# Replacing three-part low-precision products by plain float products in the first stage and in the dense expert stage

## What is computed

```python
proj = jnp.einsum('bld,dc->blc', x, w_in)
z_s, xbc, dt_pre, u_m, v_m, o_m, i_pre, f_pre = jnp.split(proj, offs, axis=-1)
xbc, new_ssd_conv = _causal_conv(xbc, st_ssd_conv, conv_ssd_w, conv_ssd_b)
xbc = jax.nn.silu(xbc)
...
u_c, new_mconv = _causal_conv(u_m, st_mconv, conv_m_w, conv_m_b)
...
def block(xb):                      # experts
    ...
    hid = jax.nn.gelu(jnp.einsum('td,thkd->thk', xb, jnp.take(u, eidx, axis=0)), approximate=False)
    return jnp.einsum('thk,thkd->td', gate * hid, jnp.take(v, eidx, axis=0))
```

## Time and profile before

| what | us |
|---|---|
| median of 3 runs | 3532.05 |
| lowest and highest | 3519.77 and 3536.51 |
| the profiled execution, time on the device | 3519.66 |
| its span from the first to the last instruction | 3517.9 |
| mean granted TensorE clock in it | 0.957 of full |

### The profile page before, as it was taken

The page is one execution under the profiler, slowest core; times in us unless marked ns, Lnnn a source line. Parts: engine busy times, 40 slices in busy tenths (PEclk is TensorE's granted clock), DMA queues, the critical chain, the costliest instruction groups (busy, mean ns, idle before and its releaser), DMA issues.

```text
span 3517.9 us, 45887 instructions
## 1 busy us (share of the span) xinstructions
PE 3159.4 (90%) x15111; PEld 2142.2 (61%) x15111; DVE 2543.4 (72%) x5323; ACT 966.6 (27%) x2280; POOL 1738.2 (49%) x1432
## 2 busy tenths in 40 slices
PE   8998998999788888888878666999999999999998
PEld 8998997878433332223234444777677767777764
DVE  6662001699586888888888995777777777777777
ACT  3112222566201111211148873111111111111111
POOL 2322221344125667766664455555555555565553
PEclk9999999899899999999989887999999999999999
DMA  3324432687857999999998999999999999999996
GB/s 110 92 82 160 161 140 93 225 295 272 313 163 253 361 345 356 362 332 341 360 332 325 338 349 364 381 394 392 392 391 398 395 376 382 397 394 389 391 378 242
DMA packets 393200, 1074.39 MB, mean 305 GB/s; under 512 B 56040, under 2 KB 158440, under 8 KB 385952
## 3 DMA queue, kind: packets, MB, share of 16 engines
q0 software_dynamic: 186624, 679.56, 51.5%
q1 hardware_dynamic: 144728, 308.27, 24.1%
q10 hardware_dynamic: 61640, 84.02, 6.6%
HBM read 978.52 MB, written 93.05 MB: 305 GB/s over the span
## 4 chain that ended last, share of the span: by engine, by line
PE 41%; DMA 11%; DVE 9%; issue 6%; POOL 4%; ACT 1%; POOLq 0%; ACTq 0%; DVEq 0%; another core or an unknown queue 0%; SPq 0%
PE PB L2138 17%; PE PB L2125 14%; DMA vbf<-in_peer_v,gixv 7%; PE PB L2165 3%; PE PB L2114 3%; DVE ub L1794 3%; PE PB L2101 2%; POOL ub L1524 2%; DMA x1d<-in_peer_u 2%; POOL vbf L1524 2%; DMA ub<-in_peer_u,gix 2%; PE PB L2209 1%; PE PB L2083 1%; DVE ohb L1741 1%; DVE oha L1739 0%
## 5 line engine op out<-in xcount | busy, mean ns | idle before, releaser
L1524 POOL DMA_INDIRECT ub<-in_peer_u,gix x640 | 692.0, 1081 | 639.8 <-DVE hid L1794 432.4
L2138 PE MATMUL PB<-vbd,wd 128*128 128x512 f32 x1536 | 685.3, 596 | 0.0
L2125 PE MATMUL PB<-xds,uts 128*128 128x384 f32 x3072 | 569.0, 340 | 0.0
L2125 PEld LDWEIGHTS PB<-xds,uts 128*128 128x128 f32 x3072 | 531.3, 189 | 0.5 <-issue 0.5
L1524 POOL DMA_INDIRECT vbf<-in_peer_v,gixv x300 | 339.7, 1132 | 279.6 <-PE PB L2165 133.1
L1524 POOL DMA_INDIRECT vbf<-in_peer_v,gix x340 | 396.9, 1167 | 163.1 <-issue 100.8
L2138 PEld LDWEIGHTS PB<-vbd,wd 128*128 128x128 f32 x1536 | 283.8, 191 | 309.9 <-issue 309.9
L2165 PE MATMUL PB<-vbf,dg 128*64 128x512 f32 x1200 | 327.1, 669 | 137.5 <-DMA vbf<-in_peer_v,gixv 130.3
L1755 DVE TENSOR_TENSOR uts<-PB,uts 128x512 fp32r<-128x512 f32 x256 | 176.0, 687 | 299.1 <-ACT uts L1971 291.5
L1794 DVE CUSTOM_DVE_ANT_0 ub<-ub,x1g 128x1024 f32<-128x1024 f32 x257 | 313.9, 1223 | 73.0 <-DMA ub<-in_peer_u,gix 60.8
L1971 ACT CAST uts<-PB 128x512 fp32r<-128x512 f32 x256 | 150.0, 586 | 641.2 <-PE PB L2114 619.3
(11 more groups left out here) (398 smaller groups left out, 5304.9 us busy)
## 6 DMA issues: line engine op xcount, KB each, us to landing
vbd<-in_peer_v SPq DMA_DIRECT2D x128, 512.0 KB
x1d<-in_peer_u SPq DMA_DIRECT2D x96, 512.0 KB
gd_d<-stag ACTq DMA_DIRECT2D x12, 2048.0 KB
gbd<-gd_d SPq DMA_DIRECT2D x16, 1536.0 KB
ubd<-in_peer_u SPq DMA_DIRECT2D x32, 512.0 KB
wtr<-in_w_tok SPq DMA_DIRECT2D x12, 1024.0 KB, 6.7
tok_d<-stg ACTq DMA_DIRECT2D x96, 128.0 KB, 1.7
rb<-rows_d SPq DMA_DIRECT2D x8, 1536.0 KB, 9.3
```

Source lines behind the costliest of these rows:

```text
L1524: pool.indirect_dma_start(out=buf, out_offset=None, in_=a[table], in_offset=bass.IndirectOffsetOnAxis(ap=index, axis=0)).then_inc(done, 16)
L2125: last = T.matmul(PB[:, 6, 0:TD], uts[:, b % 2, ul, k, :], xds[:, xl, k, :], start=(k, n) == (0, 0), stop=(k, n) == (KD - 1, 2))
L2138: last = T.matmul(PB[:, 2 * d + n, :], wd[:, b % 2, d * CH:(d + 1) * CH], vbd[b % 8][:, n * 512:(n + 1) * 512], start=b == 0, stop=b == NB ...
```

## The change

In the first stage x is loaded once into `xt` and used as it is, and the weights are used where they were loaded (`wrow`, `wcr`, `wtr`). Each product is one plain float matmul where there were three. The casts on ScalarE, the subtractions on VectorE and the splits on GpSimd are gone. Before a tile TensorE waits for the load, and SP waits for TensorE's last use of a buffer before it loads it again. SP issues the loads of x ahead of the first two channel tiles. ScalarE takes tile j out of the accumulator before it finishes tile j - 1 (`chan_in`, `chan_out`, unrolled), and the sum of the four sample parts is stored two tiles later. In the dense part `uts` holds the transposed u once, as float; `u_low` is gone from VectorE, the copy of x into a high part from ScalarE, and its low part from GpSimd; `block_u` has 8 matmuls instead of 24. The loads of the `v` blocks 4 to 7 wait for `gmm` and no longer for the split of x.

```diff
@@ first stage, SyncE
                     sp.dma_start(wrow, a["w_row"]).then_inc(s_wr, 16)
+                    for k in range(KD):
+                        sp.dma_start(xt[:, k, :], a["x_t"][:, k, :]).then_inc(s_x[k], 16)
                     for q in range(2):
                         sp.dma_start(wcr[q][:, :, :], a["w_ch"][q, :, :, :]).then_inc(s_w[q], 16)
-                    for k in range(KD):
-                        free(sp, s_xl, k - NX + 1)
-                        sp.dma_start(xst[k % NX], a["x_t"][:, k, :]).then_inc(s_x[k % NX], 16)
...
-                                sp.wait_ge(s_cp[q], i)
+                                sp.wait_ge(s_mm[q], i)
                                 sp.dma_start(wcr[q][:, :, :], a["w_ch"][2 * i + q, :, :, :]).then_inc(s_w[q], 16)
...
                     def tok_load(i, q):
-                        free(sp, s_tp[q], i)
-                        if not isinstance(i, int):
-                            sp.wait_ge(s_sm[q], i)
+                        free(sp, s_tm[(2, 5)[q]], 3 * i - 1 + q)
                         sp.dma_start(wtr[q][:, :, :], a["w_tok"][2 * i + q, :, :, :]).then_inc(s_tw[q], 16)
@@ first stage, TensorE
-                            pe.wait_ge(s_cp[q], i + 1)
+                            pe.wait_ge(s_w[q], 16 * (i + 1))
                             free(pe, s_ev[q], i)
                             for part in range(3):
                                 for k in range(KD):
-                                    for u, (x, w) in enumerate(terms((xh, xl), wch[q])):
-                                        last = nc.tensor.matmul(PB[:, 3 * q + part, 0:TN], w[:, k, :], x[:, k, part * TN:(part + 1) * TN],
-                                                                start=k == 0 and u == 0, stop=k == KD - 1 and u == 2)
+                                    last = nc.tensor.matmul(PB[:, 3 * q + part, 0:TN], wcr[q][:, k, :], xt[:, k, part * TN:(part + 1) * TN],
+                                                            start=k == 0, stop=k == KD - 1)
...
-                                    for v, (x, w) in enumerate(terms((xh, xl), wtk[q])):
-                                        last = nc.tensor.matmul(PB[:, b, 0:TW], x[:, k, t * CH:(t + 1) * CH], w[:, k, :],
-                                                                start=k == 0 and v == 0, stop=k == KD - 1 and v == 2)
+                                    last = nc.tensor.matmul(PB[:, b, 0:TW], xt[:, k, t * CH:(t + 1) * CH], wtr[q][:, k, :],
+                                                            start=k == 0, stop=k == KD - 1)
@@ first stage, ScalarE
+                    for j in range(NCT):
+                        chan_in(j)
+                        if j:
+                            chan_out(j - 1)
+                    chan_out(NCT - 1)
@@ expert stage, VectorE, ScalarE and TensorE
-                def u_low(b, x):
-                    dve.wait_ge(s["utc"], 2 * b + x + 1)
-                    V.tensor_tensor(uts[:, b % 2, 1, 4 * x:4 * x + 4, :].rearrange("p k e -> p (k e)"), PB[:, 7, :],
-                                    uts[:, b % 2, 0, 4 * x:4 * x + 4, :].rearrange("p k e -> p (k e)").bitcast(f32), ALU.subtract).then_inc(s["utl"], 1)
...
-                    S.copy(uts[:, b % 2, 0, 4 * x:4 * x + 4, :].rearrange("p k e -> p (k e)"), PB[:, 7, :]).then_inc(s["utc"], 1)
+                    S.copy(uts[:, b % 2, 4 * x:4 * x + 4, :].rearrange("p k e -> p (k e)"), PB[:, 7, :]).then_inc(s["utl"], 1)
...
                     for k in range(4 * x, 4 * x + 4):
-                        for n, (ul, xl) in enumerate(((0, 0), (0, 1), (1, 0))):
-                            last = T.matmul(PB[:, 6, 0:TD], uts[:, b % 2, ul, k, :], xds[:, xl, k, :],
-                                            start=(k, n) == (0, 0), stop=(k, n) == (KD - 1, 2))
+                        last = T.matmul(PB[:, 6, 0:TD], uts[:, b % 2, k, :], xds[:, 0, k, :], start=k == 0, stop=k == KD - 1)
```

More of the change, by code:

```diff
@@ L80, in build @@
 def build(nc, a, o):
-    f32, f32r = mybir.dt.float32, mybir.dt.float32r
+    f32 = mybir.dt.float32
     ACT = mybir.ActivationFunctionType
@@ L120, in sb @@
                 return ctx.enter_context(nc.sbuf_tensor(name, shape, dt))
-            xh, xl = (sb(n, [P, KD, NTOK], f32r) for n in ("xh", "xl"))
-            wch = [[sb(f"wch{part}{i}", [P, KD, P], f32r) for part in "hl"] for i in range(2)]
-            wtk = [[sb(f"wtk{part}{i}", [P, KD, TW], f32r) for part in "hl"] for i in range(2)]
+            xt = sb("xt", [P, KD, NTOK])
             wcr = [sb(f"wcr{i}", [P, KD, P]) for i in range(2)]
@@ L150, in build @@
             smp, ssum, xsm = sb("smp", [NSMP, 4, TW]), sb("ssum", [NSMP, TW]), sb("xsm", [P, KD, NSMP])
[L151 to L154, removed]
             wrow = wqt[0][:, :].rearrange("p (k n) -> p k n", k=KD)
             wps = [c[:, 0:KD * NK] for c in cv]
-            s_x = [sem(f"x_loaded{i}") for i in range(NX)]
-            s_xh, s_xl = sem("x_high_part"), sem("x_split")
+            s_x = [sem(f"x_loaded{i}") for i in range(KD)]
             s_wr, s_gb = sem("wrow_loaded"), sem("gate_bias_loaded")
[L161 to L164, removed]
             s_w = [sem(f"chan_weights_loaded{i}") for i in range(2)]
@@ L317, in _ @@
                 def _(act):
-                    for k in range(KD):
-                        act.wait_ge(s_x[k % NX], 16 * (k // NX + 1))
-                        nc.scalar.copy(xh[:, k, :], xst[k % NX]).then_inc(s_xh, 1)
                     act.wait_ge(s_rw, 1)
@@ L447, in _ @@
                     dve.wait_ge(s_z0, 1)
-                    for k in range(KD):
-                        dve.wait_ge(s_xh, k + 1)
-                        nc.vector.tensor_tensor(xl[:, k, :], xst[k % NX], xh[:, k, :].bitcast(f32), ALU.subtract).then_inc(s_xl, 1)
                     dve.wait_ge(s_re, 1)
@@ L1148, in build_peer @@
 def build_peer(nc, a, o, L_):
-    f32, f32r, u32 = mybir.dt.float32, mybir.dt.float32r, mybir.dt.uint32
+    f32, u32 = mybir.dt.float32, mybir.dt.uint32
     ACT = mybir.ActivationFunctionType
@@ L1251, in build_peer @@
         vbd = vbd[1:] + vbd[:1]
-        xds = sb("xds", [P, 2, KD, TD], f32r)
+        xds = sb("xds", [P, 2, KD, TD])
         vbd += [sb(f"vbd{n}", [P, D])[:, :] for n in (4, 5, 6, 7)]
@@ L1776, in _ @@
                     q, at = background(t)
-                    if t == SD:
-                        u_low(0, 0)
-                    for b in range(NBLK - 1):
-                        if block_slot(b) == t:
-                            u_low(b + 1, 1)
                     if t < U_SLOTS + NSMP:
```

126 lines of the change are left out of this document (40 added, 86 removed).

## The result

The changed kernel takes 3700.43 us (median of 4 runs, 3700.11 to 3700.76); the kernel before, measured beside it, takes 3525.91 us (4 runs, 3506.06 to 3536.51). The ratio is 1.050 with a 95% interval of 1.045 to 1.055: slower by 174.5 us. The forecast was 3710 with a range of 3680 to 3772.

The account below looks back on a forecast made before the run. TensorE's pace was taken to set the dense part and, with gaps, the first stage. The profiled 3519.7 us plus 85.1 (first stage) and 100.8 (dense part) made 3705.6, put at 3710; range 3680 to 3772.

Parts of the forecast that it names:

- 14 ns on top: Rival: plain records in all three changed products carry 14 ns above their columns' clocks, +50 us, 3760 in all; chance 0.10.
- one clock a column: Rival: plain records of all three changed products run at one clock per column, -208 us, 3316 in all; chance 0.03.
- (a): First stage, row product: plain products cost +2.6 us, an earlier TensorE start gains 3.7; together -1.1 us.
- (b): Channel tiles: 13.90 us a tile against 11.31, by 20 tiles +51.8 us.
- (c): Channel tiles: waits for GpSimd's low part and the lower clock after them go, -18.8 us.
- (d): Before the token tiles: TensorE's wait for the first token weights' low part goes, -6.1 us.
- (e): Token tiles: 3.46 us a tile against 2.84, by 96 tiles +59.3 us.
- (f): Dense part, `block_u`: 5.16 us against 4.18, by 127 blocks +124.5 us.
- (g): Dense part: VectorE loses 176 us of subtractions but isn't the bound, so nothing comes of it block by block.
- (h): Start of the dense part, gates stored to first `block_v`: shorter by between 2.1 and 13 us, taken as -10.
- (i): Dense part: TensorE's stalls waiting for blocks of u taken as gone, -13.7 us; at worst they stay.
- The transfers as the pace of the dense part: Rival: the DMA engines hold a block at 10.20 us, so `block_u` grows unseen, 3599 in all; chance 0.05.

Follow-up runs that it names:

- the kernel with four products: The kernel before with a fourth `f32r` product (low x low) per k in `block_u` of the dense part: 3681.04 us, ratio 1.044 to the kernel before.
- the halves: The kernel before with only the first stage changed, 3600.43 us (ratio 1.022), and with only the dense part changed, 3611.20 us (ratio 1.024).

## Why the prediction was right, point by point

The forecast of 3710 was 9.6 us above the measurement, and its sum, 3705.6 for a profiled execution, 4.9 above the profiled 3700.71. The mechanism held: TensorE's records set both stages, and two plain records cost more than three of `f32r`. That the sum came so near is partly luck. By the table above the first stage came out 10.9 us under its terms (-0.3, -2.0 and -8.6), and the rest 6.0 us over them (+3.1 at the start of the dense part, +1.0 behind it, +1.9 in the piece between, which had no term).

**The price of a plain product.** 289.5, 216 and 322.7 ns a record were worked out for three shapes that the trace didn't have; 289, 216 to 217.5 and 323 came. The straight line through 257 and 512 columns held. The two rivals on prices fall with it: 14 ns on top would have made a block 11.36 us, one clock a column would have left it below 10.2.

**(a)** The row product and the earlier start: -1.1 predicted, -1.4 found (first channel product at 21.5). TensorE starts at 5.48 instead of the 5.9 worked out.

**(b), (c), (d)** The channel stretch with the wait before the token tiles: 51.8 - 18.8 - 6.1 = +26.9 predicted, +24.9 found. The stretch of 277.7 us is exactly the product pace, 20 x 13.9. The size of (c) was right and its cause half right: the waits for the low part do go, but with the splits kept, ScalarE's order alone takes most of them away too. In its profile it brings the first token product 20.3 us forward, in the medians 15 us.

**(e)** The token tiles: +59.3 predicted, +50.7 found. This is the term that was mis-sized, by 8.6 us. The products cost what was said: 96 x 16 x 217.5 ns are 334.1 us against 96 x 2.84 = 272.6, +61.5. But the stretch before held 10.8 us more of other things, which I had left standing. Two rows of before, at the passage from the channel to the token tiles, and the waits there:

```profile
275.00:285.00 10.00, 9.31 (x69) 7.97 (x70) 6.38 (x5) 2.21 (x4) 7.97 (x3) 0.75 0.20 54
295.00:305.00 10.00, 6.62 (x35) 6.62 (x36) 1.94 (x1) 4.04 (x10) 0.00 (x0) 0.66 0.20 64
```
```profile
PE PB L299 <- ACTq L393: 3.5, 1, 3.5
```

TensorE waits 6.1 us for the first low part and runs on at the lower level of its clock, waits 3.5 us more for ScalarE's queue, and runs on at the lower level again; the granted clock is 0.75 and 0.66 in the two rows. The starts of the token records lie 0.213 us apart up to 280.2 and again from 298.4 to 303.9, which is 256 columns at 1.2 GHz, and 0.118 us elsewhere. In the changed kernel the same stretch is

```profile
299.00:309.00 10.00, 10.00 (x58) 8.15 (x58) 5.28 (x8) 3.28 (x5) 0.00 (x0) 1.00 0.30 86
```

with no wait and the full clock. 3.5 us of the second wait, and 2.0 and 2.5 us lost to the lower clock behind the two waits, make 8.0 of the 10.8; the rest wasn't traced. I had counted the first wait with its own 6.1 us, without the lower clock behind it, though the earlier trace rows shows that very effect elsewhere.

**(f)** `block_u`: a block of 11.18 us predicted, 11.19 found; from the first `block_v` on +110.8 predicted (124.5 - 13.7), +111.8 found.

**(g)** In the changed kernel nothing came of VectorE's 176 us block by block: a block costs what its records cost. Its wait for ScalarE's copy went over into the wait for the gelu, as was said:

```profile
DVE wd L1694 <- ACT hg L1902: 421.4, 99, 5.9
```

**(h)** The start of the dense part: -10 predicted, -6.9 found. The chain of waits shows what ends last there: the load of the gates' first blocks behind their store, both transfers, and not the u blocks.

```profile
2217.82 13.19 DMA gd_d<-stag
...
2231.08 20.90 DMA gbd<-gd_d
...
2252.00 0.57 DVE wd L1694
...
2252.70 5.39 PE PB L2059 x12
```

From the store to the first `block_v` 21.7 us pass, and 20.90 of them are this load. TensorE's own work of some 15.5 us lies beneath it, so no more than 28.6 - 20.9 = 7.7 could be gained. The step had counted only engines.

**(i)** The stalls for blocks of u: taken as gone, and all but one of 0.8 us are. In the kernel with four products, at 11.59 us a block, there are none either, and with the first stage alone changed, at 10.20, they stay: they go with the longer block. The DMA share fell to 0.95; 0.93 was predicted.

**Rivals.** The transfers as the pace of the dense part would have given 3599. They are a floor, but of some 10 us a block, under TensorE's 10.20; the change goes away from it. By the ridge of 220 operations per byte, given for bf16 (the Trainium skill, Perfetto Trace Analysis, Roofline), the dense part should have stayed at its time; it grew by all that TensorE's records grew, and the measurement decides.

**Open.** The piece between the first stage and the gates, which no edit touches, takes from some 1535 to 1568 us in the profiles, and I found no order in it. In the kernel with ScalarE's new order it took 10.7 us more, so that the 20.2 us gained by the last sample product of the token tiles (555.9 against 576.1) had shrunk to 9.5 when the gates were stored (2145.4 against 2154.95). What sets this piece wasn't settled, nor the 20 us between the sum of the halves' medians and the whole.

## What to carry to other kernels

Count a product by the clocks that its records take and not by the number of products: three `f32r` products were 18 to 19% cheaper than one plain product at the three shapes, so that fewer instructions, and some 200 us less work on each of two other engines, made the kernel 5% slower. Two resources that both stand at 100%, here TensorE and the DMA engines, can have different floors: change the work of one in both directions before you call it the bound, and expect a gain to end at the other one's floor (here 0.1 to 0.4 us below the 10.20 of a block). When the profile names an engine in a wait, follow the chain upstream and look for an in-order engine that finishes the old tile before it takes over the new one.

## What the runs showed of the hardware

A plain product of 256 to 512 columns left two records of two clocks a column and about 3 ns (217.5, 289, 323, 429 ns at 256, 344, 384, 512 columns), an `f32r` product one record of one clock a column and 12 to 14 ns (118, 157, 174 ns at 256, 344, 384) at the full clock. At the lower clock nothing stood on top: 213 ns at 256 columns. A weight load lasts some 190 ns for either kind, plain in the first row (changed kernel) and `f32r` in the second (before). It overlaps the products, since `f32r` products follow each other every 118 ns all the same:

```profile
L2059 PEld LDWEIGHTS PB<-vbd,wd x1536: 187/190/193, 2252.7 to 3671.6; 128*128 128x128 f32 x192
```
```profile
L299 PEld LDWEIGHTS PB<-wtkh,xh x768: 186/188/330, 277.5 to 598.8; 128*128 128x128 f32 x192
```

What was new to me: a wait of TensorE of 2.3 us costs more than itself, since the granted clock is lower in the stretch behind it (6.85 instead of 5.15 us for the next `block_v`; 0.66 and 0.75 over the 10 us around the end of waits of 3.5 and 6.1 us); and five kernels with the same first-stage instructions showed one of two patterns in it, some 13 us apart.
